# Trainium2 encoder kernel: the first three pairs of FFN 0 in four contraction quarters, with the modulation sums taken as columns

## What the kernel computes

```python
cond = jax.nn.silu(c)
mod = (cond @ ada_w[layer] + ada_b[layer]).reshape(B_, N_MOD, D)      # D = 1024, N_MOD = 9
sh1, sc1, g1, sh2, sc2, g2, sh3, sc3, g3 = [mod[:, i] for i in range(N_MOD)]
h = modulate(rmsnorm(x, norm_g[layer, 0]), sh1, sc1)                  # h * (1 + sc1) + sh1
x = x + 0.5 * g1[:, None, :] * swiglu(h, ff_w13[layer, 0], ff_w2[layer, 0])
# swiglu: a, b = split(h @ w13); (silu(a) * b) @ w2, with D_FF = 2816; 256 tokens
```

## Time and profile before

| | before |
|---|---|
| time, 3 runs | 941.64 to 942.1 us, median 941.72 us |
| span of the profiled execution | 939.9 us (its own device time is not shown; the median is 1.8 us above the span) |
| PE busy | 916.3 us, 97% |
| DVE busy | 712.6 us, 76% |
| ACT busy | 456.9 us, 49% |
| moved by DMA | 239.25 MB, mean 255 GB/s |

### The profile page before, as it was taken

How to read it: one execution, slowest core, us unless ns; L and a number is a source line. 1 busy time by engine, 2 the same in 40 slices (tenths; PEclk the granted TensorE clock), 3 DMA queues, 4 the chain that set the end, 5 groups by cost and what they waited for, 6 DMA issues and landing times.

```text
span 939.9 us, 11106 instructions
## 1 busy us (share of the span) xinstructions
PE 916.3 (97%) x4300; PEld 749.1 (80%) x4300; DVE 712.6 (76%) x720; ACT 456.9 (49%) x637; POOL 111.1 (12%) x177
## 2 busy tenths in 40 slices
PE   3899999999999999999999999999999999999998
PEld 1588888888877888888888888888888888888886
DVE  4987988986979867878888678778777888553544
ACT  1374344245766848344244474353564483443421
POOL 1101111201522100111111001101200110000000
PEclk9999999999999999999999999999999999999999
DMA  9999998797655648999999459986776498555221
GB/s 313 376 360 379 364 346 298 256 316 190 229 174 178 208 156 278 331 331 330 350 325 328 156 184 313 318 288 226 258 274 198 154 336 298 179 188 171 90 89 46
DMA packets 147444, 239.25 MB, mean 255 GB/s; under 512 B 14528, under 2 KB 106432, under 8 KB 147264
## 3 DMA queue, kind: packets, MB, share of 16 engines
q1 hardware_dynamic: 127664, 169.10, 53.8%
q0 software_dynamic: 18864, 69.21, 20.4%
q10 hardware_dynamic: 864, 0.23, 0.1%
HBM read 237.48 MB, written 1.05 MB: 254 GB/s over the span
## 4 chain that ended last, share of the span: by engine, by line
PE 93%; DVE 3%; DMA 1%; issue 1%; ACT 1%; POOL 0%; SPq 0%; DVEq 0%; POOLq 0%; ACTq 0%
PE ps L1704 58%; PE ps L1824 8%; PE ps L1829 8%; PE ps L1825 8%; PE ps L1789 2%; DMA ada<-in_ada_w 1%; PE ps L2111 1%; PE ps L1696 1%; PE ps L1839 1%; PE ps L1847 1%; DVE xn L1250 1%; PE ps L2059 0%; DVE x L1254 0%; PE ps L2091 0%; PE ps L2075 0%
## 5 line engine op out<-in xcount | busy, mean ns | idle before, releaser
L1704 PE MATMUL ps<-hi,hT_hi 128*128 128x512 f32 (+1 forms) x804 | 317.0, 394 | 0.8 <-DVE hT_hi L1298 0.8
L1704 PE MATMUL ps<-hi,hT_lo 128*128 128x512 f32 (+1 forms) x804 | 312.2, 388 | 0.0
L1704 PE MATMUL ps<-lo,hT_hi 128*128 128x512 f32 (+1 forms) x788 | 305.4, 388 | 0.0
L1116 DVE TENSOR_TENSOR lo<-raw,hi 128x2048 fp32r<-128x2048 f32 (+1 forms) x74 | 164.6, 2229 | 24.9 <-ACT hi L719 24.8
L1704 PEld LDWEIGHTS ps<-hi,hT_hi 128*128 128x128 f32 x804 | 151.1, 188 | 31.9 <-issue 2.6
L1704 PEld LDWEIGHTS ps<-hi,hT_lo 128*128 128x128 f32 x804 | 150.9, 188 | 31.5 <-DVE hT_lo L1301 0.2
L1704 PEld LDWEIGHTS ps<-lo,hT_hi 128*128 128x128 f32 x788 | 148.2, 188 | 29.2 <-issue 0.2
L719 ACT ACTIVATE hi<-raw 128x2048 fp32r<-128x2048 f32 (+1 forms) x73 | 138.1, 1892 | 22.0 <-DMA raw<-in_ff_w 19.8
L611 POOL DMA_DIRECT2D ada<-in_ada_w x128 | 69.0, 539 | 473.9 <-DVE acc L1176 184.0
L1176 DVE SCALAR_TENSOR_TENSOR acc<-ada,cond,acc 128x1024 f32<-128x1024 f32 x70 | 89.7, 1281 | 7.6 <-DMA ada<-in_ada_w 4.2
L1116 DVE TENSOR_TENSOR lo<-arena,hi 128x2048 fp32r<-128x2048 f32 x31 | 70.9, 2289 | 14.5 <-ACT hi L719 14.4
(11 more groups left out here) (227 smaller groups left out, 1166.9 us busy)
## 6 DMA issues: line engine op xcount, KB each, us to landing
ada<-in_ada_w POOLq DMA_DIRECT2D x128, 512.0 KB, 6.5
raw<-in_ff_w SPq DMA_DIRECT2D x55, 1024.0 KB, 7.8
raw<-in_ff_w SPq DMA_DIRECT2D x88, 512.0 KB, 6.5
arena<-in_ff_w SPq DMA_DIRECT2D x31, 1024.0 KB, 7.2
raw<-in_w_in SPq DMA_DIRECT2D x12, 1024.0 KB, 5.1
arena<-in_ada_w SPq DMA_DIRECT2D x4, 1024.0 KB, 13.0
raw<-in_w_out SPq DMA_DIRECT2D x4, 1024.0 KB, 5.9
ada<-in_ada_w SPq DMA_DIRECT2D x2, 1024.0 KB, 8.3
```

The costliest lines, as they stand in the source:

```text
L1116: ins = V.tensor_tensor(lo, src, hi.bitcast(F32), ALU.subtract)
L1704: ins = mm(out, a, b, start=first and m == 0, stop=last and m == len(pairs) - 1, skip_group_check=shared)
```

## The change

The first three pairs of FFN 0 (0, 2, 1 in the order of `FIRST_ORDER`) are worked together, in four quarters `q` of the contraction: quarter q holds contraction tiles 2q and 2q+1. For each quarter SP loads the 256 columns of shift and scale that belong to it (four transfers of 0.5 MB) and three units of w13 (0.5 MB each, one for each pair). DVE sums all 8 tiles of shift and scale side by side in one 512-wide instruction a tile (`first_tile(q, j)`; in quarter 0 PE takes tiles 1, 3, 5, 7). PE brings the partitions together by matmuls whose stationary operand is the 128x128 block and whose moving operand is one column (`ones` for `acc`, `cond` for PE's own tiles), which leaves the sum as a column in bank 3 (`first_sum`). So the row products, `add_row`, the transposes of `acc` and the reductions are gone. x is transposed first and copied to SBUF by ACT without modulation; each quarter is modulated when its columns are there, high part on ACT (`first_high`), full value and low part on DVE (`first_low`). The second pair of the three uses PSUM banks 0 and 1 for its result, which are `w2`'s output banks, so its gate product must be read before `w2(0)` starts.

```diff
-ADA_COUNT = [{2: 3, 3: 4, 4: 5, 5: 5, 6: 5, 7: 6, 8: 6, 9: 6}, {p: 5 for p in range(2, 10)},
+ADA_COUNT = [{3: 5, 4: 5, 5: 6, 6: 6, 7: 6, 8: 6, 9: 6}, {p: 5 for p in range(2, 10)},
+FIRST, QUARTERS = 3, 4
+FIRST_ORDER = (0, 2, 1)
+PE_TILES = ((1, 3, 5, 7), (), (), ())
+TURN_BANK, SUM_BANK = (2, 6, 7, 0), 3
...
+def pair_bank(f, p):
+    return 0 if (f, p) == (0, 2) else 4 + 2 * ((PAIRS * f + p) % 2)
...
+# SP
             sp.dma_start(x[:, 0, :], x_v[:, 0, :]).then_inc(x_in_sem, 16)
             sp.dma_start(x[:, 1, :], x_v[:, 1, :]).then_inc(x_in_sem, 16)
+            for q in range(QUARTERS):
+                if q == 3:
+                    sp.wait_ge(first_used, tiles_summed(1))
+                    sp.wait_ge(mod_ps, 1)
+                load_first(q)
+                for i in range(FIRST):
+                    if (q, i) == (2, 1):
+                        sp.wait_ge(first_used, tiles_summed(2))
+                        sp.wait_ge(mod_ps, 2)
+                    load_unit(q, i)
+            for q in range(4):
+                load_w2(0, q)
...
+# ACT
+            def first_high(q):
+                act.wait_ge(first_acol, q + 1)
+                act.wait_ge(x_copied, q + 1)
+                for kk in range(2):
+                    j = 2 * q + kk
+                    nc.scalar.activation(hT_hi[:, j, :], turned_pair(q, kk), ACT.Identity, bias=modc[:, 0, j:j + 1],
+                                         scale=acol[:, 0, j:j + 1]).then_inc(hhi_done, 2)
             norm_squares(0, 0)
             norm_squares(0, 1)
+            for q in range(QUARTERS):
+                act.wait_ge(xT_done, q + 1)
+                nc.scalar.activation(x_turned[:, 2 * q:2 * q + 2, :].rearrange("p j n -> p (j n)"),
+                                     ps[:, TURN_BANK[q], :], ACT.Copy).then_inc(x_copied, 1)
+            for q in range(QUARTERS):
+                unit_high(q, 0)
+                first_high(q)
+                for i in range(1, FIRST):
+                    unit_high(q, i)
+            w2_high(0)
+            silu(0, 0)
+            w2_high(1)
+            u_high(0, 0)
+            silu(0, 2)
+            split_hi(2 * FIRST)
+            silu(0, 1)
...
+# DVE
+            for q in range(QUARTERS):
+                first_columns(q)
+                first_low(q)
+                unit_low(q, 0)
+                unit_low(q, 1)
+                if q < QUARTERS - 1:
+                    for j in summed_tiles(q + 1):
+                        first_tile(q + 1, j)
+                unit_low(q, 2)
+            w2_low(0)
+            u_mul(0, 0)
+            w2_low(1)
+            u_low(0, 0)
+            u_mul(0, 2)
+            split_lo(2 * FIRST)
+            u_mul(0, 1)
...
+# PE
+            def first_pairs():
+                first_sum(0, True, False)
+                first_turn()
+                first_sum(0, False, True)
+                for q in range(QUARTERS - 1):
+                    for i in range(FIRST):
+                        unit_first(q, i)
+                    for i in range(FIRST - 1):
+                        unit_second(q, i)
+                    first_sum(q + 1, True, True)
+                    unit_second(q, FIRST - 1)
+                for i in range(FIRST):
+                    unit_first(QUARTERS - 1, i)
+                    if i == FIRST - 1:
+                        u_transpose(0, 0)
+                    unit_second(QUARTERS - 1, i)
...
+                    first_pairs()
+                    pe.wait_ge(u_done, u_done_at(0, 2))
                     w2(0)
+                    u_transpose(0, 1)
                     w2(1)
+                    w2(2)
+                    w2(3)
```

More of the change, by code:

```diff
@@ L90, in plan_slots @@
             before.append(POOL_PIECES[0] - 2)
+            continue
+        if n < 2 * FIRST:
+            slot.append(n)
+            before.append(-1)
+            last[n] = n
             continue
@@ L170, in h32_count, with split_count, summed_tiles, tiles_summed @@
 def h32_count(s, t, j):
-    if s == 0:
-        return 8 * ((j - 1) // 4) + 4 * t + (j - 1) % 4 + 1
-    return 16 * (s - (s == 5)) + 8 * t + j
+    return 16 * (s - 1 - (s == 5)) + 8 * t + j
 def piece_of(f, p, half):
-    if f == 0 and p < 2:
-        return 2 * half + p
+    if f == 0 and p < FIRST:
+        return FIRST * half + FIRST_ORDER[p]
     return 2 * (FFN_PAIR[f] + p) + half
[L184 to L201, removed]
+def split_count(n):
+    return n - 2 * FIRST + 1
+def summed_tiles(q):
+    return [j for j in range(KT) if j not in PE_TILES[q]]
+def tiles_summed(q):
+    return sum(len(summed_tiles(i)) for i in range(q))
 def columns_summed(g):
@@ new lines, in first_low @@
+            def first_low(q):
+                dve.wait_ge(first_acol, q + 1)
+                dve.wait_ge(x_copied, max(q + 1, 4))
+                for kk in range(2):
+                    j = 2 * q + kk
+                    V.tensor_scalar(x_mod[:, j, :], turned_pair(q, kk), acol[:, 0, j:j + 1], modc[:, 0, j:j + 1],
+                                    ALU.mult, ALU.add).then_inc(first_mod, 1)
+                dve.wait_ge(first_mod, 2 * q + 2)
+                dve.wait_ge(hhi_done, 4 * q + 4)
+                both = slice(2 * q, 2 * q + 2)
+                V.tensor_tensor(hT_lo[:, both, :], x_mod[:, both, :], hT_hi[:, both, :].bitcast(F32), ALU.subtract
+                                ).then_inc(hlo_done, 4)
@@ L1327, in ffn @@
                         ada_tile(*tile)
[L1328 to L1330 removed]
+                    split_lo(n0 + 2 * p + (2 if p else 3))
                     if p:
@@ L1757, in w13 @@
                 n = piece_of(f, p, half)
-                if f == 0 and p < 2:
-                    w13_first(p, half, tiles, between)
-                    return
-                pe.wait_ge(lo13_done, n + 1)
+                pe.wait_ge(lo13_done, split_count(n))
                 wh, wl = (v.rearrange("p (m k c) -> p m k c", m=2, k=4) for v in unit_src(n)[1])
@@ L1840, in mod_half @@
                 ins.then_inc(mod_ps, 1)
-            def first_row(half, g, tiles):
-                last = ROW_TILES[half][g]
-                for j in tiles:
-                    w = first_weights(pe, half, g, j)
-                    ins = mm(ps[0:1, row_bank(half, g), :], cond[:, j:j + 1], w, start=j == last[0], stop=j == last[-1])
-                    if j == last[-1]:
-                        ins.then_inc(first_rows, 1)
-            def first_sum(half, g):
-                pe.wait_ge(row_added, rows_done(half, g))
-                mod_half(g, half, row_bank(half, g))
             def split_sum(g, half, bank):
```

379 lines of the change are left out of this document (185 added, 194 removed).

## The result

| | before | the change |
|---|---|---|
| time, median (range, runs) | 941.91 us (941.64 to 943.2, 4) | 946.8 us (946.21 to 948.56, 4) |
| span of the profiled execution | 939.9 us | 944.4 us (its own time 946.21) |
| pair 3's first w13 product, in PE's order of time | 80.81 us | 85.26 us |
| from there to the end of the span | 859.1 us | 859.1 us |

A forecast was written before the change was run, and what follows sets the result against it. PE, busy 97% of the span, was the bound, with idle time at the start. First column 18.6, three quarters of 12.0 and the rest put pair 3 at 78.7 against 80.97; 941.7 - 2.3 = 939.4 us, range 936.0 to 943.2.

The forecast's parts named there:

- PE before the first scale column: From the weights' landing at 12.9 to the column sum at 18.6, PE's work and hand-over take 5.7 us.
- The first weights: At the start, the first weights land at 12.9 us, between 12.0 and 13.5, against 14.15 before.
- My upper bound of 9 us for PE behind the landing: PE's work from the landing to the first column sum takes 9 us if all runs at half clock.
- the hole in the transfers: DMA engines only 49% busy at 8 to 9 us; part may close, landing at 12.0 if gone.
- A quarter on DVE: Each of the first three quarters lasts 12.0 us, bound by DVE; PE needs 9.2, ACT 4.2.
- The two new waits: Behind quarter 3, PE waits about 1.2 us before `w2(0)` and about 1.1 before `u_transpose(0, 1)`.
- Later pairs: Later pairs with 6 vector tiles cost 0; rival: DVE late in pairs 5 to 7, 3 us, 942.5, chance 0.07.
- Late start at half clock: Rival: PE's start takes 9 instead of 5.7 us, column sum at 21.9, 942.7 at the worst; chance 0.27.
- The clock falls in every quarter: Rival: PE's waits for DVE in quarters 0 to 2 bring half clock; 943 to 951 us, chance 0.13.

The follow-up runs named there:

- e5: The changed kernel with 38 products of 512 moving columns on PE ahead of its first wait for weights; 946.55 us.
- e8: e6 with 26 wide products of ones on PE ahead of the transposes of x; 941.85 us.
- e7: e6 with the six small transfers issued only behind the norm of x; 942.09 us.
- e10: e9 with PE taking one of the eight vector tiles in each of quarters 1 to 3; 940.08 us.
- e4: The changed kernel with `silu` and `u_mul` of the second and third pair put ahead of what stood before them; 945.21 us.
- e3: The changed kernel with x scaled and transposed ahead of the first vector sum; 944.47 us.
- e6: The changed kernel with the edits of e2, e3 and e4 together; 942.50 us.
- e9: e7 with DVE's wait for `adab` and `ngT` moved from ahead of the first vector sum to behind it; 939.59 us.
- e11: e10 with 13 wide products of ones on PE between the transposes of x and the first column sum; 938.51 us.
- e12: The kernel before the change, with its six small transfers issued behind the squares of x; 941.54 us.
- e1: The changed kernel with 80 products 128x128 of ones on PE ahead of its first wait for weights; 952.43 us.
- e2: The changed kernel with all 8 tiles of quarter 0 summed by DVE, none by PE; 944.68 us.

## Why the prediction was wrong

The forecast was 939.4 us, 2.3 faster; it came out 4.9 slower. In the profile pair 3 was forecast at 78.7 and came at 85.26, 6.6 us off: 5.0 up to the first column, 1.1 in the three quarters, and 0.45 behind them.

- **The step that failed: PE before the first scale column.** I had 5.7 us from the landing of the weights at 12.9 to the column sum at 18.6, priced at the full clock. From the first landing at 12.09 to the column at 23.60 PE worked without a pause for 11.5 us, nearly all of it at half clock. Three things were wrong. (1) The price: 0.25 us for a matmul (two rows) holds at the full clock, where e5 shows 0.24, but the sixteen ran at half clock, 0.43 each, 6.8 us. (2) The overlap: I put eight of them beside the transfers. At the full clock they do fit there (e5: the first eight took 1.92 us from 12.02, the second landing came at 14.93); at 0.43 each they don't, so all 16 were on the path, 6.8 us where I had 2.0. (3) The transposes took 3.44 us until the next group, not 2.43. I read the 2.43 of before as 0.15 for each, but that was an average over two clocks. In the windows below the first 1 us holds 5 of them and a later one 12 (the last partly): after the four row products and some five transposes the full clock had come. In e8 they took 0.13 each behind wide products; elsewhere in the changed kernel and its variants the sixteen took 3.50 to 3.65 us.

The transposes of x alone in the kernel before (line 1696; length, busy of PE and PEld, clock, DMA, GB/s):

```profile
17.80:18.80 1.00, 1.00 (x5) 1.00 (x6) 1.00 1.05 379
18.90:19.90 1.00, 1.00 (x12) 1.00 (x10) 1.00 1.09 352
```

- **The first weights.** Second landing 12.9 forecast, 13.5 at the latest; it came at 14.9 (e5's wait, and the changed kernel's own issue at 3.6 us with 11.3 to land). It was hidden behind PE's slow rows. Had PE been at the full clock, it would have been the bound: 14.93 and 1.9, 2.4, 0.95 and 0.3 of PE's work give about 20.5, still 1.9 above the forecast. That is worked out, not measured. By it 3.1 of the 5.0 us are the clock and 1.9 the landing. My upper bound of 9 us for PE behind the landing holds if it is counted from there (23.60 - 14.93 = 8.7); counted from 12.9 it was too low. I took it that the hole in the transfers might close; it got deeper (83 and 57 GB/s), and e7 shows that the small transfers on ACT's and POOL's queues make it.
- **A quarter on DVE.** 12.0 forecast, 12.34, 12.59 and 12.18 measured, 1.1 us in all. Half of it is the 0.51 in quarter 2, whose cause is open. DVE bounds the quarters as said; e10 shows it directly, 0.84 off DVE is 0.84 off the quarter.
- **The two new waits.** 1.2 and 1.1 forecast, 1.08 and 0.88 measured, at the instructions named. e4 takes both away and gives 1.6 us at the median. This loss was seen in advance, and it could have been avoided by the order of four instructions. The stretch from quarter 3's column to pair 3 still took 24.55 us against 24.1: PE's own work in it was 0.8 longer than my sum, the waits 0.34 shorter.
- **Later pairs.** 0 forecast, 0.1 measured. That rival falls.
- **Late start at half clock** was the rival that came true, with its price too low: 21.9 at the worst against 23.60, so its 942.7 was too low as well. It had the same landing at 12.9 as the forecast.
- **The clock falls in every quarter** (the rival that ended at 943 to 951). The time of 946.8 lies in its range, but for another reason. Its pattern is there, in two of the three quarters: PE busy for 0.56 of 2 us at 46 to 48, and the clock at 0.55 at 50 to 52; and 0.58 at 26 to 28. The Trainium skill, TensorE: Matmul & The Clock Gate, section on HAM oscillation, describes it for a kernel whose bursts stand 3 to 5 us apart; here, behind a wait of 1.97 us, the trace agrees that it happens, but in the changed kernel it lengthened no quarter. DVE never waited for PE's sum there, so slow matmuls fell into time that PE had anyway. It was close: in e3, e4, e6 and e9 DVE waited 0.2 to 0.7 us for PE's sum in one or two quarters, and where DVE was given less (e10, quarter 1), the same half clock did become the bound, for 2.30 us.

What the change set out to do it did in part. The row products are gone, but PE's idle time is not: up to pair 3, and without the wait for the first weights, its waits over 0.25 us add up to 6.6 us where they were 3.6. The same four quarters with the start and the end put right (e9 to e11) are 0.2 to 0.4% faster than before, and e12 shows that the late transfers alone would not have given that. The time was lost around the quarters, not by them.

## What to carry to other kernels

Work put on an engine that has not run yet must be priced at the speed of a cold start, and from the landing of its own data: compare the same instruction at the start and in mid-run, and ask what stood ahead of it in the row that you take the price from. A product with one moving column is not small: with its 128x128 stationary block a row of it took as long as a product with 128 columns (0.217 us at the lower clock), so 32 of them may cost more than the vector instructions that they replace. Before giving up on a restructured stage, separate its terms with single edits; here three small edits, the placing of six small transfers and one moved wait (e9) took 7.2 us off the changed kernel.

## What the runs showed of the hardware

- A float32 product with one moving column is two rows, each 0.217 us at 1.2 GHz and 0.12 at 2.4 GHz; an fp32r product with 128 moving columns also took 0.217 at the lower clock (e1).
- 80 products of 128 columns, 17.3 us without a gap, ran at 0.217 each to the end, and what followed was as slow (e1). Behind 38 products of 512 columns (10.4 us) the same rows ran at 0.12 (e5), and behind 13 the column sum took 1.05 instead of 1.86 us (e11). Width alone doesn't decide it: behind the 16 transposes of x, 128 columns each and 3.65 us in all, the column sum took 1.05 us in e2 and the fill ran at the full clock in e11, while in e3 the rows right behind the same transposes stayed at 0.217. What makes the difference is not shown.
- The clock column read 1.00 in stretches at the start where the rows lasted twice as long. I would not trust it before the first change that it shows.
- Six small transfers, 225 KB in all, made a hole in the large ones (83 and 57 GB/s at 7 to 9 us, 350 without them, e7); without it DVE's first sum started 1.8 us earlier (e9). `ngT`, 24 KB, landed 8.3 us after its issue in the changed kernel, when x, 512 KB a piece, took 4.4.
